# Newton steps and query rotation of the latent heads moved from VectorE to GpSimd, and half of a projection moved ahead of twelve transposes

## The chip, the cores and the metric

The kernel runs on one core of one Trainium2 chip. The metric is the device time of one execution in microseconds. Its engines have the profile's names: PE is TensorE, DVE is VectorE, ACT is ScalarE, POOL is GpSimd, SP issues the loads.

## What is computed

A trunk of two layers over 512 tokens of 1,024 features, all in float32. Layer 0 has two attentions side by side (differential attention, "A", with 4 heads, and latent attention, "B", with 8 heads), layer 1 has stick-breaking attention with 16 heads, and each layer ends with a SwiGLU network. The change lies in layer 0. Cut to that:

```python
a_q, a_k, a_v, b_ql, b_kvl, b_kr = split_cols(h @ w_in, AB_IN_SPLITS)
a_q = rope(rms_norm(a_q.reshape(B, S, 2 * A_HEADS, A_QK_DIM), a_q_norm), pos)
a_k = rope(rms_norm(a_k.reshape(B, S, 2 * A_HEADS, A_QK_DIM), a_k_norm), pos)
...
q_b = (rms_norm(b_ql, b_q_a_norm) @ b_w_q_b).reshape(B, S, B_HEADS, B_NOPE_DIM + B_ROPE_DIM)
kv_b = (rms_norm(b_kvl, b_kv_a_norm) @ b_w_kv_b).reshape(B, S, B_HEADS, B_NOPE_DIM + B_V_DIM)
q_nope, q_rope = q_b[..., :B_NOPE_DIM], q_b[..., B_NOPE_DIM:]
k_nope, b_v = kv_b[..., :B_NOPE_DIM], kv_b[..., B_NOPE_DIM:]
q_nope = rms_norm(q_nope, b_q_nope_norm)
k_nope = rms_norm(k_nope, b_k_nope_norm)
q_rope = rope(rms_norm(q_rope, b_q_rope_norm), pos)
out_b = latent_attention(q_nope, q_rope, k_nope, k_rope, b_v, (B_NOPE_DIM + B_ROPE_DIM) ** -0.5)
```

`rms_norm` divides by the root of a mean square, `rope` turns pairs of elements by an angle that depends on the token. B's q has 64 elements without rotation and 32 with it, per head.

## The kernel before

**Matmuls in three passes.** Every float32 operand is held as a rounded part (`_hi`) and a rest (`_lo`), and a product is hi*hi + hi*lo + lo*hi. The weights come in chunks g = 0, 1, 2, ...: SP loads a chunk into `wraw`, ACT writes `w_hi` (`hi_static`, line 318), POOL writes the rest `w_lo` (`lo(g)`, line 330), PE reads both. There are three slots, so ACT may split chunk g once PE is done with g-3 (a semaphore count), and SP may load chunk g once `w_lo` of g-3 is written. Chunks 4 and 5 are A's first q projection, 6 to 9 are B's two up-projections, 10 to 19 are A's other projections.

**Order.** The order of each engine is written out by hand, and engines meet by semaphores. An engine that waits holds back all that stands behind it. PE's order in layer 0 is: the latents (`lat_pe`), the first half of A's first projection (`pj_pe(pe, 0, 0, i)`, i counts four blocks of 128 tokens), twelve transposes of the normalised latents (`lat_trans_pe`, line 732, which wait for DVE's `latn`), the second half (`pj_pe(pe, 0, 1, i)`), then B's projections `bq_pe` and `bkv_pe` for heads 0 to 3 and again for heads 4 to 7, A's second projection `pj_pe(pe, 1, ...)` with the transposes of head 0's q and k between its halves (`b_qk_pe`, lines 1112 and 1119). Then comes a loop over the eight latent heads u: scores (`b_scores_pe`, line 1037), transposes of q and k of head u+1, three quarters of a half projection for A, transposes of the probabilities (line 1017), the last quarter, and values (line 1088). Then follow the four heads of A (scores at line 1167), the output projection, the network and layer 1.

**Beside it, in a head.** DVE takes the row maxima (`b_max_dve`, line 1050), ACT the exponentials (line 1054), DVE three reciprocals (`b_inv_dve`, line 1060), ACT scales the probabilities (line 1066) and splits q and k of the next head, DVE writes their rests (`b_qk_dve`) and those of the transposed probabilities (`b_pt_dve`, line 1080). `qk_dve` (lines 964 to 967) turns A's projections out of PSUM, t = 0 and t = 1 being the two banks; PE's next projection waits for its line 966 before it writes the same bank. `b_mean_dve` and `qk_mean_dve` (line 987) write mean squares.

**Norm factors.** 1/sqrt(m) is Ln and Exp on ACT (`rs_act`) and one Newton step on DVE, three small instructions (`rs_newton_dve`, lines 400, 402, 404). All norms share the scratch columns `T_M`, `T_Y` and `T_A` of `tiny`. The fourteen norms are numbered by `ROOT`, in order lat, b0, b1, q0, k0, k1, q1, o0, ...

**Pairs of latent heads.** B's q and k are scaled and q is turned for two heads at a time, before PE transposes them. `b_pair_dve` (lines 884 to 892) has five DVE instructions for the rotated 32 columns of q: two products with the sine table into `t2b`, one with the cosine table in place, a sum and the scale. `b_pair_pool` (line 905) has two POOL instructions for the 64 plain columns of q and of k. Pair 0 stands before the loop, pair n+1 at the end of DVE's work for head u = 2n, that is ahead of the maxima of head u+1:

```python
for c in range(3):
    b_pt_dve(dve, u, c)
...
if u % 2 == 0 and u < 6:
    b_pair_dve(dve, u // 2 + 1)
```

PE waits for both halves of a pair in `b_qk_pe`, right behind the scores of head 2n+1.

Of the kernel before, what the change touches and what calls it, by code (L numbers as in the profile page):

```python
# [140 lines left out]
def trunk(nc, xt, w_ab, w_in, w_down, mats, masks_a, masks_c, tabs, rows, vecs, out):  # L141
# [728 lines left out]
    def b_pair_dve(dve, pr):  # L870

        hf, h, z = pr // 2, 2 * pr, Z_B[pr // 2] + 8 * (pr % 2)
        dve.wait_ge(S("rs_root"), ROOT[f"b{hf}"] + 1)
# [15 lines left out]
        dve.wait_ge(S("b_rope"), 4 * pr + 3)
        nc.vector.tensor_tensor(q[:, :, :, c:B_QK], q[:, :, :, c:B_QK], t, ALU.add).then_inc(S("b_rope"), 1)  # L890
        dve.wait_ge(S("b_rope"), 4 * pr + 4)
        nc.vector.tensor_tensor(q[:, :, :, c:B_QK], q[:, :, :, c:B_QK], root(32, B_ROPE),
                                ALU.mult).then_inc(S("b_qk"), 1)

    def b_pair_pool(pool, pr):

# [1387 lines left out]
```

## Time and profile before

| what | value |
|---|---|
| median of three runs | 1336.61 us (1335.61 to 1336.84) |
| the profiled execution, its time | 1336.34 us |
| its span in the trace | 1334.5 us |
| PE busy | 1281.6 us (96%) |
| DVE, ACT, POOL busy | 598.0, 574.6, 514.0 us |
| mean granted clock of PE | 0.986 of full speed |

Times in the text are microseconds from the start of the span. A matmul's busy time overlaps its neighbour's, so PE's pace is read from the distance of two starts. The stretches are: latents and first projections to 75.9, the eight latent heads from there to 190.9, A's heads and the output projection to about 300, and the rest of the kernel, untouched by the change.

### The profile page before, as it was taken

What the parts mean: (1) busy time and instruction counts of PE and PEld (TensorE: products, weight loads), DVE (VectorE), ACT (ScalarE), POOL (GpSimd) and SP (SyncE); (2) the same over time, 40 slices, a digit from 0 to 9 for tenths busy, and PEclk for the clock granted to TensorE, in tenths of its full rate; (3) what the DMA queues carried; (4) which work ended last, traced back from release to release, by engine and by line L of the source; (5) the groups of instructions that cost most, each with busy time, mean ns of one, the idle gap of its engine ahead of it and who ended that gap; (6) DMA issues with size and microseconds to landing.
All of it is one profiled execution on the core that took longest, in us unless ns stands there. A gap on an engine that the chain in (4) does not pass through costs nothing.

```text
span 1334.5 us, 16920 instructions
## 1 busy us (share of the span) xinstructions
PE 1281.6 (96%) x6308; PEld 1076.2 (81%) x6308; DVE 598.0 (45%) x1033; ACT 574.6 (43%) x953; POOL 514.0 (39%) x223
## 2 busy tenths in 40 slices
PE   8888898999999999999989999998999999999999
PEld 8788887778888888888868888886888888888887
DVE  7877777753221112222168888887222220122210
ACT  5656665643332122233366777776333331222310
POOL 5432411164445434445522222221644453344441
PEclk9889998999999999999989999999999999999999
DMA  5220111022223222233111111110323332233331
GB/s 207 72 64 33 33 47 33 16 91 95 95 101 115 84 79 94 94 118 103 65 62 48 47 63 47 49 61 17 104 88 98 98 122 89 71 98 100 102 129 40
DMA packets 29143, 105.84 MB, mean 79 GB/s; under 512 B 3360, under 2 KB 3616, under 8 KB 29088
## 3 DMA queue, kind: packets, MB, share of 16 engines
q1 hardware_dynamic: 28944, 105.07, 23.9%
q8 instruction: 37, 0.61, 0.2%
q14 instruction: 18, 0.15, 0.0%
q10 hardware_dynamic: 144, 0.02, 0.0%
HBM read 102.98 MB, written 2.10 MB: 79 GB/s over the span
## 4 chain that ended last, share of the span: by engine, by line
PE 66%; DVE 17%; ACT 10%; issue 5%; POOL 1%; DMA 0%; ACTq 0%; DVEq 0%; SPq 0%; POOLq 0%
PE bank L342 19%; PE bank L343 19%; PE bank L346 19%; DVE cs_hi L1477 2%; DVE cs_lo L1479 2%; ACT ca L1435 1%; ACT ca L1433 1%; ACT w_hi L318 1%; ACT cq_hi L1516 1%; DVE pt_lo L1080 1%; POOL ssum L436 1%; ACT pn L1066 1%; ACT pn L1054 1%; DVE cs L1445 1%; DVE tiny L1185 1%
## 5 line engine op out<-in xcount | busy, mean ns | idle before, releaser
L330 POOL TENSOR_TENSOR w_lo<-wraw,w_hi 128x1024 fp32r<-128x1024 f32 (+4 forms) x180 | 458.6, 2549 | 751.8 <-ACT w_hi L318 751.8
L342 PE MATMUL bank<-h_hi,w_hi 128*128 128x512 f32 x896 | 353.8, 395 | 1.0 <-DVE h_lo L426 1.0
L343 PE MATMUL bank<-h_lo,w_hi 128*128 128x512 f32 x896 | 351.6, 392 | 0.0
L318 ACT ACTIVATE w_hi<-wraw 128x1024 fp32r<-128x1024 f32 (+4 forms) x180 | 197.3, 1096 | 158.2 <-DVE x L633 128.7
L346 PE MATMUL bank<-h_hi,w_lo 128*128 128x512 f32 x896 | 223.4, 391 | 0.0
L342 PEld LDWEIGHTS bank<-h_hi,w_hi 128*128 128x128 f32 x896 | 168.9, 188 | 38.6 <-DVE h_lo L426 1.6
L346 PEld LDWEIGHTS bank<-h_hi,w_lo 128*128 128x128 f32 x896 | 168.3, 188 | 37.0
L343 PEld LDWEIGHTS bank<-h_lo,w_hi 128*128 128x128 f32 x896 | 168.9, 189 | 36.0
L342 PE MATMUL bank<-f_hi,w_hi 128*128 128x512 f32 x352 | 138.3, 393 | 0.0
L343 PE MATMUL bank<-f_lo,w_hi 128*128 128x512 f32 x352 | 138.3, 393 | 0.0
L619 DVE TENSOR_TENSOR fu<-bank,rstd 128x512 f32<-128x512 f32 x44 | 30.4, 691 | 200.3 <-PE bank L346 200.3
L633 DVE TENSOR_TENSOR x<-bank,x 128x512 f32<-128x512 f32 x32 | 22.1, 692 | 202.2 <-PE bank L346 202.2
L596 ACT ACTIVATE f_hi<-fa 128x512 f32 (+1 forms) x44 | 27.8, 632 | 195.6 <-DVE fa L622 195.6
L592 ACT ACTIVATE fs<-fy 128x512 f32<-128x512 f32 x44 | 27.8, 632 | 138.3 <-DVE fy L617 138.3
L346 PE MATMUL bank<-f_hi,w_lo 128*128 128x512 f32 x352 | 86.4, 393 | 0.0
L343 PEld LDWEIGHTS bank<-f_lo,w_hi 128*128 128x128 f32 x352 | 66.2, 188 | 15.0
L346 PEld LDWEIGHTS bank<-f_hi,w_lo 128*128 128x128 f32 x352 | 66.2, 188 | 15.0
L342 PEld LDWEIGHTS bank<-f_hi,w_hi 128*128 128x128 f32 x352 | 66.2, 188 | 14.9
L617 DVE TENSOR_TENSOR fy<-bank,rstd 128x512 f32<-128x512 f32 x44 | 30.4, 691 | 104.6 <-PE bank L346 104.1
L930 PE MATMUL bank<-w_hi,h_hi 128*128 128x256 f32 x192 | 57.6, 300 | 5.2 <-DVE ka L966 4.8
L932 PE MATMUL bank<-w_hi,h_lo 128*128 128x256 f32 x192 | 55.5, 289 | 0.0
L934 PE MATMUL bank<-w_lo,h_hi 128*128 128x256 f32 x192 | 55.5, 289 | 0.0
(272 smaller groups left out, 2015.9 us busy)
## 6 DMA issues: line engine op xcount, KB each, us to landing
wraw<-in_w_in SPq DMA_DIRECT2D x120, 512.0 KB, 3.3
wraw<-in_w_down SPq DMA_DIRECT2D x32, 704.0 KB, 4.1
wraw<-in_w_ab SPq DMA_DIRECT2D x20, 512.0 KB, 3.3
x<-in_xt SPq DMA_DIRECT2D x8, 256.0 KB, 6.9
out<-x SPq DMA_DIRECT2D x8, 256.0 KB, 2.0
wraw<-in_w_ab SPq DMA_DIRECT2D x4, 416.0 KB, 6.8
wraw<-in_w_ab SPq DMA_DIRECT2D x2, 384.0 KB, 3.1
wraw<-in_w_ab SPq DMA_DIRECT2D x2, 256.0 KB, 2.9
```

The costliest lines, as they stand in the source:

```text
L318: nc.scalar.activation(whi[:, s, 0:width], wraw[:, s, 0:width], ACT.Copy).then_inc(S("w_hi"), 1)
L330: nc.gpsimd.tensor_tensor(wlo[:, s, 0:width], wraw[:, s, 0:width], whi[:, s, 0:width], ALU.subtract).then_inc(S("w_lo"), 1)
L342: nc.tensor.matmul(out_bank, w, src_hi[kt], start=(kt == 0), stop=False)
L343: nc.tensor.matmul(out_bank, w, src_lo[kt], start=False, stop=False)
L346: last = nc.tensor.matmul(out_bank, wlo[:, s, kt * P:(kt + 1) * P], src_hi[kt], start=False, stop=(kt == n - 1))
L592: nc.scalar.activation(fs[:], fy[:], ACT.Silu).then_inc(S("net_s"), 1)
L596: nc.scalar.activation(tile_at(f_of[L][0], f), as3(fa[:], f), ACT.Copy).then_inc(S("net_hi"), 1)
L617: nc.vector.tensor_tensor(fy[:], bank[2 * j][:], rstd[:], ALU.mult).then_inc(S("net_y"), 1)
L619: nc.vector.tensor_tensor(fu[:], bank[2 * j + 1][:], rstd[:], ALU.mult).then_inc(S("net_u"), 1)
L930: nc.tensor.matmul(o, tok(hhi, 4 * c + k, i), whi[:, slot(g), w], start=(c == 0 and k == 0 and i % 2 == 0), stop=False, skip_group_check=True)
L932: nc.tensor.matmul(o, tok(hlo, 4 * c + k, i), whi[:, slot(g), w], start=False, stop=False, skip_group_check=True)
L934: last = nc.tensor.matmul(o, tok(hhi, 4 * c + k, i), wlo[:, slot(g), w], start=False, stop=(c == 1 and k == 3), skip_group_check=True)
```

## The change

Three edits. GpSimd makes the Newton step of b0, b1, q0, k0, k1 and q1, in four instructions instead of three. GpSimd does the five instructions for q's rotation, in front of the two that it did already. PE runs the token blocks 0 and 1 of the second half of A's first projection ahead of the latents' transposes. With this, the steps get new places on POOL and DVE: on POOL, pair 0 comes before chunk 11's `w_lo` as it did, pairs 1 to 3 now come before chunk 14, 16 and 18 instead of behind them; on DVE, in heads 2 and 4 (and 6 for `va_dve`) the step for A's projection stands behind the first of the three reciprocals instead of behind the third. The writers of the means wait until the Newton step before theirs is done, since they share the scratch columns.

```diff
...
     def rs_newton_dve(dve, name, n, at):
         r = ROOT[name]
         m, y, a = (tiny[:, t:t + n] for t in (T_M, T_Y, T_A))
+        n_before = 2 * (r if r < ROOT["b0"] else r - len(POOL_ROOTS))
         dve.wait_ge(S("rs_exp"), r + 1)
+        wait(dve, "rs_root", r)
...
+    POOL_ROOTS = ("b0", "b1", "q0", "k0", "k1", "q1")
+
+    def rs_newton_pool(pool, name, n, at):
+        r, i = ROOT[name], 3 * POOL_ROOTS.index(name)
+        m, y, a = (tiny[:, t:t + n] for t in (T_M, T_Y, T_A))
+        pool.wait_ge(S("rs_exp"), r + 1)
+        pool.wait_ge(S("rs_root"), r)
+        nc.gpsimd.tensor_tensor(a, m, y, ALU.mult).then_inc(S("rs_pool"), 1)
+        pool.wait_ge(S("rs_pool"), i + 1)
+        nc.gpsimd.tensor_tensor(a, a, y, ALU.mult).then_inc(S("rs_pool"), 1)
+        pool.wait_ge(S("rs_pool"), i + 2)
+        nc.gpsimd.tensor_scalar(a, a, -0.5, 1.5, ALU.mult, ALU.add).then_inc(S("rs_pool"), 1)
+        pool.wait_ge(S("rs_pool"), i + 3)
+        nc.gpsimd.tensor_tensor(tiny[:, at:at + n], a, y, ALU.mult).then_inc(S("rs_root"), 1)
...
     def b_mean_dve(dve, hf):
         dve.wait_ge(S("bq_sum"), NB * hf + NB)
         dve.wait_ge(S("bk_sum"), NB * hf + NB)
+        dve.wait_ge(S("rs_root"), ROOT[f"b{hf}"])
...
     def b_pair_pool(pool, pr):
...
+        wait(pool, "b_rope", 4 * pr)
...
+        nc.gpsimd.tensor_tensor(t[:, :, :, 0:s], q[:, :, :, c + s:B_QK], tab(B_ROPE, s), ALU.mult).then_inc(S("b_rope"), 1)
+        nc.gpsimd.tensor_tensor(t[:, :, :, s:B_ROPE], q[:, :, :, c:c + s], tab(B_ROPE + s, s),
+                                ALU.mult).then_inc(S("b_rope"), 1)
+        pool.wait_ge(S("b_rope"), 4 * pr + 2)
+        nc.gpsimd.tensor_tensor(q[:, :, :, c:B_QK], q[:, :, :, c:B_QK], tab(0, B_ROPE), ALU.mult).then_inc(S("b_rope"), 1)
+        pool.wait_ge(S("b_rope"), 4 * pr + 3)
+        nc.gpsimd.tensor_tensor(q[:, :, :, c:B_QK], q[:, :, :, c:B_QK], t, ALU.add).then_inc(S("b_rope"), 1)
+        pool.wait_ge(S("b_rope"), 4 * pr + 4)
+        nc.gpsimd.tensor_tensor(flat(qb, c, B_QK), flat(qb, c, B_QK), root(32, B_ROPE), ALU.mult).then_inc(S("b_qk"), 1)
+        nc.gpsimd.tensor_tensor(flat(qb, 0, c), flat(qb, 0, c), root(0, c), ALU.mult).then_inc(S("b_nope"), 1)
+        nc.gpsimd.tensor_tensor(flat(kb, 0, c), flat(kb, 0, c), root(16, c), ALU.mult).then_inc(S("b_nope"), 1)
...
             lo(10)
+            rs_newton_pool(pool, "b0", 48, Z_B[0])
             b_pair_pool(pool, 0)
-            for g in range(11, 14):
-                lo(g)
+            lo(11)
+            rs_newton_pool(pool, "b1", 48, Z_B[1])
+            lo(12)
+            lo(13)
 
             for u in range(B_HEADS):
-                lo(14 + u)
                 if u % 2 == 0 and u < 6:
                     b_pair_pool(pool, u // 2 + 1)
+                lo(14 + u)
+                if u == 1:
+                    rs_newton_pool(pool, "q0", 16, Z_Q)
...
-                for c in range(3):
-                    b_inv_dve(dve, u, c)
+                b_inv_dve(dve, u, 0)
                 if u in (2, 4):
                     qk_dve(dve, 1 + u // 2, 1)
                 if u == 6:
                     va_dve(dve, 4, 1)
+                for c in range(1, 3):
+                    b_inv_dve(dve, u, c)
...
-                if u % 2 == 0 and u < 6:
-                    b_pair_dve(dve, u // 2 + 1)
...
+            for i in range(2):
+                pj_pe(pe, 0, 1, i)
             pe.wait_ge(S("lam_exp"), 1)
             lat_trans_pe(pe)
-            for i in range(NB):
+            for i in range(2, NB):
                 pj_pe(pe, 0, 1, i)
```

What this makes of the order on POOL, from chunk 10's `w_lo` to chunk 13's, before (line 905 is the pair's two scales):

```order
L330 TENSOR_TENSOR w_lo<-wraw,w_hi 128x1024
L905 TENSOR_TENSOR qb<-qb,tiny 128x8x64
L905 TENSOR_TENSOR kb<-kb,tiny 128x512
L330 TENSOR_TENSOR w_lo<-wraw,w_hi 128x1024 x4
L905 TENSOR_TENSOR qb<-qb,tiny 128x8x64
```

and now (lines 415 to 421 are a Newton step, 907 to 917 a pair):

```order
L330 TENSOR_TENSOR w_lo<-wraw,w_hi 128x1024
L415 TENSOR_TENSOR tiny<-tiny 128x48
L417 TENSOR_TENSOR tiny<-tiny 128x48
L419 TENSOR_SCALAR tiny<-tiny 128x48
L421 TENSOR_TENSOR tiny<-tiny 128x48
L907 TENSOR_TENSOR t2b<-qb,tbq 128x8x16
L908 TENSOR_TENSOR t2b<-qb,tbq 128x8x16
L911 TENSOR_TENSOR qb<-qb,tbq 128x8x32
L913 TENSOR_TENSOR qb<-qb,t2b 128x8x32
L915 TENSOR_TENSOR qb<-qb,tiny 128x8x32
L916 TENSOR_TENSOR qb<-qb,tiny 128x8x64
L917 TENSOR_TENSOR kb<-kb,tiny 128x512
```

Nine more instructions stand between chunk 10's `w_lo` and chunk 11's, which PE needs for the half projection behind head 0's transposes.

On DVE, between the last rest of head 0's probabilities (`b_pt_dve`) and the maxima of head 1, before:

```order
L1080 TENSOR_TENSOR pt_lo<-bank,pt_hi 128x384 [waits h_phi] x2
L884 TENSOR_TENSOR t2b<-qb,tbq 128x8x16 [waits bq_ev,rs_root]
L885 TENSOR_TENSOR t2b<-qb,tbq 128x8x16
L888 TENSOR_TENSOR qb<-qb,tbq 128x8x32 [waits b_rope]
L890 TENSOR_TENSOR qb<-qb,t2b 128x8x32 [waits b_rope]
L892 TENSOR_TENSOR qb<-qb,tiny 128x8x32 [waits b_rope]
L1050 TENSOR_REDUCE tiny<-bank 128x2 [waits h_s]
```

and now:

```order
L1092 TENSOR_TENSOR pt_lo<-bank,pt_hi 128x512 [waits h_phi]
L1092 TENSOR_TENSOR pt_lo<-bank,pt_hi 128x384 [waits h_phi] x2
L1062 TENSOR_REDUCE tiny<-bank 128x2 [waits h_s]
L1113 TENSOR_TENSOR mixed_lo<-bank,mixed_hi 64x512 [waits h_mhi]
L1062 TENSOR_REDUCE tiny<-bank 128x1 [waits h_s] x2
```

The maxima of head 1 have nothing of the pair ahead of them any more.

## Rows read from the trace of the kernel before

**Rows 1.** The page, part 1: busy time, share of the span, instructions.
```profile
PE 1281.6 (96%) x6308; PEld 1076.2 (81%) x6308; DVE 598.0 (45%) x1033; ACT 574.6 (43%) x953; POOL 514.0 (39%) x223
```

**Rows 2.** Waits of PE, 60 to 191: total us, times, longest us.
```profile
PE bank L1112 <- DVE qb L892: 5.9, 3, 3.8
PE bank L930 <- DVE ka L966: 4.8, 2, 2.6
PE bank L818 <- DVE vb_lo L858: 2.4, 1, 2.4
```

**Rows 3.** Timeline of PE: start, us, instruction, idle before and its releaser.
```profile
35.98 2.79 PE L732 MATMUL bank<-mat,latn 128*128 128x128 f32 x12 [3.18 <-DVE latn L712]
94.54 1.09 PE L1112 MATMUL bank<-mat,qb 128*96 128x128 f32 x4 [3.76 <-DVE qb L892]
```

**Rows 4.** Busy time by stretch; behind POOL's: granted PE clock, DMA share, GB/s.
```profile
36.00:41.80 5.80, 5.80 (x28) 5.80 (x29) 4.47 (x11) 3.66 (x6) 3.09 (x2) 0.50 0.15 47
60.90:63.30 2.40, 0.04 (x2) 0.00 (x1) 2.33 (x9) 1.50 (x6) 2.01 (x3) 1.00 0.49 140
94.50:99.70 5.20, 5.16 (x25) 4.99 (x26) 2.71 (x8) 4.51 (x14) 0.00 (x0) 0.50 0.00 0
145.80:147.90 2.10, 2.10 (x13) 2.10 (x13) 0.54 (x2) 0.87 (x2) 0.00 (x0) 0.56 0.00 0
```

**Rows 5.** Timeline of PE: chunk 11's start; first scores of heads 0, 1, 7, A.
```profile
70.34 0.37 PE L930 MATMUL bank<-w_hi,h_hi 128*128 128x256 f32 x1
...
75.88 0.28 PE L1037 MATMUL bank<-bk_hi,bq_hi 96*128 96x256 f32 x1
...
88.19 0.28 PE L1037 MATMUL bank<-bk_hi,bq_hi 96*128 96x256 f32 x1
...
177.25 0.28 PE L1037 MATMUL bank<-bk_hi,bq_hi 96*128 96x256 f32 x1
...
190.91 0.28 PE L1167 MATMUL bank<-ak_hi,aq_hi 128*128 128x256 f32 x1
```

**Rows 6.** Timeline of DVE: a step of b0's Newton, a sum, pair 1.
```profile
58.87 2.30 DVE L402 TENSOR_TENSOR tiny<-tiny 128x48 f32<-128x48 f32 x1
...
78.03 0.68 DVE L967 TENSOR_REDUCE tiny<-pj_sq 128x8 f32<-128x512 f32 x1
...
87.16 2.48 DVE L885 TENSOR_TENSOR t2b<-qb,tbq 128x128 f32<-128x128 f32 x1
89.67 1.15 DVE L888 TENSOR_TENSOR qb<-qb,tbq 128x256 f32<-128x256 f32 x1
...
92.04 2.45 DVE L892 TENSOR_TENSOR qb<-qb,tiny 128x256 f32<-128x256 f32 x1
```

**Rows 7.** Timeline of POOL.
```profile
58.64 2.46 POOL L330 TENSOR_TENSOR w_lo<-wraw,w_hi 128x1024 fp32r<-128x1024 f32 x1 [3.11 <-ACT w_hi L318]
61.49 1.04 POOL L905 TENSOR_TENSOR qb<-qb,tiny 128x512 f32<-128x512 f32 x1 [0.39 <-DVE tiny L404]
...
77.75 2.38 POOL L330 TENSOR_TENSOR w_lo<-wraw,w_hi 128x1024 fp32r<-128x1024 f32 x1 [6.82 <-ACT w_hi L318]
86.90 2.59 POOL L330 TENSOR_TENSOR w_lo<-wraw,w_hi 128x1024 fp32r<-128x1024 f32 x1 [6.77 <-ACT w_hi L318]
...
90.50 1.22 POOL L905 TENSOR_TENSOR kb<-kb,tiny 128x512 f32<-128x512 f32 x1
```

**Rows 8.** POOL's groups by shape, 0 to 300: busy us, mean ns, idle before.
```profile
L1628 POOL TENSOR_TENSOR tq<-rawt,rawg 128x512 f32<-128x512 f32 x1 | 1.3, 1295 | 0.0
...
L1628 POOL TENSOR_TENSOR tbq<-rawt,rawg 128x256 f32<-128x256 f32 x1 | 0.7, 717 | 0.0
```

**Rows 9.** Timeline of DVE and ACT where A's first projection is turned.
```profile
43.77 0.42 DVE L964 TENSOR_TENSOR t<-bank,tq 128x256 f32<-128x256 f32 x1 [1.59 <-ACT pj_sq L945]
...
45.04 0.68 DVE L967 TENSOR_REDUCE tiny<-pj_sq 128x8 f32<-128x512 f32 x1
...
47.50 0.49 ACT L833 ACTIVATE bq_sq<-bank 128x384 f32<-128x384 f32 x1
```

More of the change, by code:

```diff
@@ L868, in b_mean_dve, with b_pair_pool @@
                                        spread(col(T_EPS), [P, 16]), ALU.mult, ALU.add).then_inc(S("rs_mean"), 1)
-    def b_pair_dve(dve, pr):
+    def b_pair_pool(pool, pr):
         hf, h, z = pr // 2, 2 * pr, Z_B[pr // 2] + 8 * (pr % 2)
-        dve.wait_ge(S("rs_root"), ROOT[f"b{hf}"] + 1)
-        dve.wait_ge(S("bq_ev"), NB * hf + NB)
+        pool.wait_ge(S("rs_root"), ROOT[f"b{hf}"] + 1)
+        pool.wait_ge(S("bq_ev"), NB * hf + NB)
+        pool.wait_ge(S("bk_ev"), NB * hf + NB)
+        wait(pool, "b_rope", 4 * pr)
         q = qb[:, h:h + 2, :, :]
@@ L889, in b_pair_dve @@
[L889 to L897, printed above, removed]
-        hf, h, z = pr // 2, 2 * pr, Z_B[pr // 2] + 8 * (pr % 2)
-        pool.wait_ge(S("rs_root"), ROOT[f"b{hf}"] + 1)
-        pool.wait_ge(S("bq_ev"), NB * hf + NB)
-        pool.wait_ge(S("bk_ev"), NB * hf + NB)
-        for t, at in ((qb, 0), (kb, 16)):
-            o = t[:, h:h + 2, :, 0:B_NOPE].rearrange("p h i n -> p (h i) n")
-            nc.gpsimd.tensor_tensor(o, o, spread(col(z + at, 8).rearrange("p (j o) -> p j o", o=1), [P, 8, B_NOPE]),
-                                    ALU.mult).then_inc(S("b_nope"), 1)
+            return spread(col(z + at, 8).rearrange("p (j o) -> p j o", o=1), [P, 8, n])
@@ new lines, in flat @@
+        def flat(t, a, b):
+            return t[:, h:h + 2, :, a:b].rearrange("p h i n -> p (h i) n")
+        nc.gpsimd.tensor_tensor(t[:, :, :, 0:s], q[:, :, :, c + s:B_QK], tab(B_ROPE, s), ALU.mult).then_inc(S("b_rope"), 1)
+        nc.gpsimd.tensor_tensor(t[:, :, :, s:B_ROPE], q[:, :, :, c:c + s], tab(B_ROPE + s, s),
+                                ALU.mult).then_inc(S("b_rope"), 1)
+        pool.wait_ge(S("b_rope"), 4 * pr + 2)
+        nc.gpsimd.tensor_tensor(q[:, :, :, c:B_QK], q[:, :, :, c:B_QK], tab(0, B_ROPE), ALU.mult).then_inc(S("b_rope"), 1)
@@ L984, in qk_mean_dve @@
         dve.wait_ge(S("pj_sum"), 2 * p + 2)
+        dve.wait_ge(S("rs_root"), ROOT[GROUPS[p]])
         e, n = ((T_EQ, A_DIM * A_SCALE ** 2), (T_E, A_DIM))[p // 2]
@@ L1300, in a_omean_dve @@
         dve.wait_ge(S("a_l0"), u + 1)
+        dve.wait_ge(S("rs_root"), ROOT[f"o{u}"])
         nc.vector.scalar_tensor_tensor(col(T_M, NB), bank[TRK][:, 0:NB], 1.0 / (2 * A_DIM), col(T_L0, NB), ALU.mult,
@@ L1643, in _ @@
             lo(10)
+            rs_newton_pool(pool, "b0", 48, Z_B[0])
             b_pair_pool(pool, 0)
-            for g in range(11, 14):
-                lo(g)
+            lo(11)
+            rs_newton_pool(pool, "b1", 48, Z_B[1])
+            lo(12)
+            lo(13)
             for u in range(B_HEADS):
-                lo(14 + u)
                 if u % 2 == 0 and u < 6:
                     b_pair_pool(pool, u // 2 + 1)
+                lo(14 + u)
+                if u == 1:
+                    rs_newton_pool(pool, "q0", 16, Z_Q)
+                elif u in (3, 5):
+                    rs_newton_pool(pool, ("k0", "k1")[u // 4], 16, Z_K + 16 * (u // 4))
+                elif u == 7:
+                    rs_newton_pool(pool, "q1", 16, Z_Q + 16)
                 if u == 0:
@@ L1933, in _ @@
                     b_pt_dve(dve, u, c)
[L1934 to L1938 removed]
+                if u == 6:
                     qk_mean_dve(dve, 1)
[L1940 to L1942 removed]
                 if u in (1, 3):
```

18 lines of the change are left out of this document (2 added, 16 removed).

## The prediction

> **What bounds the kernel now.** I read the page's first part, then PE's waits by stretch, then the timelines of the engines around each wait. PE is busy 96% of the span [rows 1], so a gain can only come from its idle time, and from stretches in which its clock is at half. The reader is to see in [rows 2] that PE lost 13.1 us in the stretch of the latent heads and just before it to three causes, all on DVE: q's rotation 5.9 (line 892), the bank of A's projection 4.8 (line 966), and B's values 2.4 (line 858). Another 3.18 went at 32.8, where the transposes wait for the normalised latents [rows 3]. A long wait costs more than itself: after those of 3.18 and 3.76 [rows 3] PE ran for 5.8 and 5.2 us at a granted clock of 0.50, its lower level of 1.2 GHz, and did half the work it could have: 2.9 and 2.6 us lost. After the wait of 2.4 the clock had stayed at 1.00; a stretch at 0.56 near 146 cost some 0.9 [rows 4].
>
> Why DVE is late is in [rows 6, 7]. Pair 1's step at line 885 took 2.48 us and ended at 89.64, when POOL's `w_lo` (86.90 + 2.59 = 89.49) was done. Line 888 took 1.15 beside POOL's scale, line 892 took 2.45. A step of b0's Newton took 2.30 and ended at 61.17, POOL's instruction at 61.10. So a DVE instruction with both inputs in SBUF is held until the running POOL instruction ends. The maxima of head 1 wait behind all that.
>
> **Edit 1: Newton and rotation leave DVE.** DVE loses four pairs (pair 1 took from 87.16 or sooner to 92.04 + 2.45 = 94.49, 7.3 us) and six Newton steps, of which one instruction alone took 2.30 [rows 6]. What comes instead on POOL: the tables give 1.295 us for 512 columns and 0.717 for 256 [rows 8], so 2.26 ns a column and 0.14 fixed. The rotation is 2 x 0.43 (128 columns) and 3 x 0.72 (256), 3.0, and with three waits on itself (estimate 0.13 each) 3.4. The two scales were there (1.04 each, [rows 7]), so a pair takes 5.5. A Newton step of 48 columns is 4 x 0.25 plus waits, 1.5.
>
> Where it lies on the path, place by place.
>
> *Before head 0.* Chunk 10's `w_lo` ends at 61.10 [rows 7]. Then come Newton 1.5 (62.6), pair 0 5.5 (68.1) and chunk 11's `w_lo` 2.4: PE may start chunk 11 at 70.5. It started it at 70.34 [rows 5]. So what PE wins of the 2.4 us at 60.9, since DVE has b0's step no more, it waits for on POOL: **+0.2**. This term hangs on POOL alone, and the rotation is in it in full. Bounds: -0.5, if the patterns of 16 columns run at the rate of the scales, and +3, if they are twice as dear as the tables.
>
> *Pair 1.* It starts after chunk 13's `w_lo` (77.75 + 2.38 = 80.1, [rows 7]) and ends at 85.6. PE asks for it at 94.54 - 3.76 = 90.8 [rows 3]: 5.2 us to spare. Pairs 2 and 3 start behind the Newton step of an odd head, and are asked for behind the scores of the next odd one, with more to spare. So no wait on the rotation is left, and the chunks of `w_lo` behind the pairs are used a head later.
>
> *The heads.* From head 0 to A's first scores it took 190.91 - 75.88 = 115.0 us [rows 5]. Head 0, with no real wait, took 88.19 - 75.88 = 12.3, the last 13.7. With seven heads at 12.3 and the last at 13.7, less 0.5 for DVE's late start into it (POOL held q1's Newton too), it is 86.1 + 13.2 = 99.3: 15.7 us less. The waits and the half clock, added up another way, give 5.9 + 4.8 + 2.6 + 0.9 = 14.2, and restarts and maxima that came late make the rest. What is late next: in heads 2 and 4 A's turning (lines 964 to 967, 45.72 - 43.77 = 1.95 us, [rows 9]) now stands ahead of two reciprocals, and ACT's scaling waits for them, just before PE wants the probabilities. I put 0.3 a head and keep 0.9 for three heads (bounds 0 and 4). The term is **-14.8**, bounds -15.7 and -10.
>
> The added waits of DVE for a Newton step on POOL (`b_mean_dve`, `qk_mean_dve`, `a_omean_dve`) come at least a head after that step; b1's mean waits for b0's step, done by 62.6, some 3 us before its sums are. I cost them at nothing. If POOL's step is late there, ACT, which waits for the mean, is held with all that stands behind it.
>
> **Edit 2: two token blocks ahead of the transposes.** A half projection took 75.88 - 70.34 = 5.5 us [rows 5], so half of one is 2.8, and fills the wait of 3.18 [rows 3] but for 0.4. The clock should stay up, the transposes take half of their 2.79, and PE is done with the projection at 36.0 + 1.4 + 2.8 = 40.2, some 5 us sooner, and with the first two blocks of `bq_pe` (12 matmuls of 384 columns, 0.17 each) at 42.3. The third waits for ACT's square (line 833, 47.50 + 0.49, [rows 9]). ACT gets there behind the second square of A's projection, which shares a buffer with the first and so waits for DVE's line 967 (45.72). DVE can do its four steps 1.59 sooner [rows 9], perhaps 2, so ACT's square ends near 46.2 instead of 47.99. PE then has waited 3.9 us, as long as the waits after which its clock fell. At half clock the next 5 us of matmuls cost 2.6, which eats the 1.8 and more, of which ACT's queue hides some. The term is **+0.4**, bounds -2.3 (clock stays up) and +1. The wait is moved, not removed.
>
> Loads: DMA and SP are off the path, chunk 14 is loaded after chunk 11's `w_lo` at 70.5 and its own `w_lo` starts at 86.90 [rows 7], so nothing hangs on SP's queue. Past 191 nothing changes but the start.
>
> **Sum.** +0.2 - 14.8 + 0.4 = -14.2 on the profiled execution's own 1336.34. The median of the runs is 1336.61, 0.27 higher; the same change on it gives **1322.4**.
>
> **Where a rule speaks against it.** The rows have DVE and POOL exclude each other: POOL's own scale went from 1.04 alone to 1.22 beside DVE's rotation [rows 7]. The Trainium skill (Perfetto Trace Analysis, Optimizing Scalar/DVE Operations) says that moving operations between these two might not help, because they share an SBUF read port. It would have the term of the heads mostly gone. Its page on SBUF (SBUF — State Buffer, Who interferes with whom) says that only DVE instructions with two SBUF inputs or in a two-port mode collide. By that, little is left on DVE to collide with, and the trace agrees: line 967, one SBUF input, took 0.68 beside POOL's `w_lo` at 77.75 and 0.68 without POOL at 45.04 [rows 6, 7, 9].
>
> **The rivals.**
> - *The wait moves with the work.* POOL, held by what DVE still does in SBUF and twice as slow a column, has pairs 1 to 3 ready no sooner than DVE had. Then the 5.9 us on line 892 and the 2.6 of half clock stay: -14.2 + 8.5 = -5.7, 1330.9. For it: POOL is the slower engine. Against it: 5.2 us to spare at pair 1. The skill's first rule above would end here.
> - *The clock stays up* in the wait at 42.2, or the wait is shorter than I work out: up to 2.7 more (from +0.4 to -2.3), 1319.7. For it: 2.4 us did not lower it. Against it: after 3.18 and 3.76 it was down.
> - *GpSimd becomes the bound (slower).* No row shows POOL on patterns of two heads by four tokens by 16 columns. If each such instruction costs e/5 more than I put, pair 0 passes all of e on to chunk 11, pair 1 what exceeds 5.2, pairs 2 and 3 what exceeds about 7, and waits as long as those in [rows 3] bring the half clock, 2.6 each. At e = 7.5 (a rotation instruction of 2.1 us instead of 0.6) the gain is used up. At e = 9 it is 9 + 3.8 + 4 + 5.2 = 22 against 14.2: 1344. Against it: the scales, in 8 rows of 64, are faster than the tables.
> - *Nothing changes*, because another engine takes the place of each wait: 1336.6. ACT and DVE are busy 43% and 45% of the span [rows 1], so it would have to come from the order, not from load.
>
> **Numbers.** Forecast 0.72, clock up 0.14, wait moves 0.08, GpSimd bound 0.04, nothing 0.02. The likeliest gives 1322.4. The range takes in the bounds of the forecast's terms to both sides without adding all of them up: low 1317.5 (clock up, no new wait in the heads, 0.5 at chunk 11), high 1328.5 (+3 at chunk 11 and 3 to 4 in the heads). A measurement of this kernel can tell about 0.2%, 2.7 us, from no change. Faster 0.94, same 0.02, slower 0.04.
>
> **What would show it.** In the changed profile: no wait of PE at the transposes of q (line 1112's successor) and at most traces of one on A's bank; heads 12.3 us apart, A's first scores near 177; a new wait of some 3.8 us in `bq_pe` near 42 with a clock of 0.50 behind it; chunk 11 started by PE near 70.5 right after POOL's `w_lo`; POOL's rotation instructions at 0.43 and 0.72. The prediction is wrong if a rotation instruction takes over 1.5 us, if the reciprocals behind A's turning hold the probabilities by more than 1 us a head, or if maxima are late for another reason.

## The result, and the profile after

The changed kernel took 1316.83 us (median of four runs, 1315.25 to 1319.36), the kernel before 1336.11 beside it: a ratio of 0.986 (95% interval 0.984 to 0.988), so faster by about 19 us. Two later series of the same kernel gave medians of 1319.3 and 1318.44, and the median of all twelve of its runs is 1318.44, so the first four lay low. The forecast was 1322.4, its range began at 1317.5.

The page, part 1, beside [rows 1]:

```profile
PE 1277.3 (97%) x6308; PEld 1073.8 (81%) x6308; DVE 567.6 (43%) x995; ACT 574.5 (44%) x953; POOL 529.4 (40%) x267
```

DVE lost 30.4 us of busy time, POOL gained 15.4. Twice as much came off one engine as went onto the other, and a good part of it was no work: the profile counts an instruction that is held as busy (2.48 us for one in [rows 6] whose like takes 0.28). The 13.1 us of waits of [rows 2] come down to two rows, by the timeline of PE (start, us, instruction, idle before and its releaser). All its rows with an idle time over 0.2 us from 30 to 165 are these:

```profile
35.54 1.50 PE L749 MATMUL bank<-mat,latn 128*128 128x128 f32 x12 [0.36 <-DVE latn L729]
45.57 0.69 PE L822 MATMUL bank<-w_hi,ql_hi 128*128 128x384 f32 x1 [3.71 <-ACT bq_sq L850]
...
62.32 0.50 PE L835 MATMUL bank<-w_hi,kvl_hi 128*128 128x512 f32 x1 [1.50 <-DVE vb_lo L875]
69.92 0.38 PE L941 MATMUL bank<-w_hi,h_hi 128*128 128x256 f32 x1 [0.32 <-POOL w_lo L330]
```

The wait at the transposes went from 3.18 [rows 3] to 0.36 and came back as 3.71 ahead of `bq_pe`'s third block. The one on B's values went from 2.4 to 1.50. Nothing is left on q's rotation, nor on A's bank. Clock and load by stretch (behind POOL's: granted clock, DMA share, GB/s), as in [rows 4]:

```profile
36.00:42.00 6.00, 5.86 (x46) 5.54 (x44) 5.09 (x11) 3.43 (x6) 3.18 (x2) 1.00 0.25 64
46.00:50.00 4.00, 4.00 (x15) 3.86 (x15) 1.66 (x7) 1.34 (x4) 0.65 (x1) 0.50 0.38 131
```

The stretch at the lower level (1.2 GHz) moved from behind the first wait to behind the second. POOL, from chunk 10's `w_lo` to chunk 11's, answers to [rows 7]:

```profile
58.54 2.40 POOL L330 TENSOR_TENSOR w_lo<-wraw,w_hi 128x1024 fp32r<-128x1024 f32 x1 [3.62 <-ACT w_hi L318]
60.90 0.28 POOL L415 TENSOR_TENSOR tiny<-tiny 128x48 f32<-128x48 f32 x1
...
61.95 0.28 POOL L421 TENSOR_TENSOR tiny<-tiny 128x48 f32<-128x48 f32 x1
62.31 0.46 POOL L907 TENSOR_TENSOR t2b<-qb,tbq 128x128 f32<-128x128 f32 x1
...
64.08 0.74 POOL L913 TENSOR_TENSOR qb<-qb,t2b 128x256 f32<-128x256 f32 x1
64.90 0.62 POOL L915 TENSOR_TENSOR qb<-qb,tiny 128x256 f32<-128x256 f32 x1
...
67.48 2.39 POOL L330 TENSOR_TENSOR w_lo<-wraw,w_hi 128x1024 fp32r<-128x1024 f32 x1
```

The Newton step took 1.41 us from start to start, the pair 5.17 (62.31 to 67.48). PE starts chunk 11 at 69.92, when POOL is done (69.87), so this place does hang on POOL. From chunk 10's `w_lo` to chunk 11's start it is 11.38 us, against 11.70 before. A's first scores:

```profile
173.92 0.28 PE L1179 MATMUL bank<-ak_hi,aq_hi 128*128 128x256 f32 x1
```

They started at 190.91 [rows 5], 16.99 later. From here to the end it is 1143.58 us, before it was 1143.59. Head 0's first scores are at 75.49 (75.88 in [rows 5]). Those 0.4 us are not the change's. A's first projection, which starts ahead of everything that was changed, already starts 0.45 sooner in this trace (timeline of PE, the kernel before, then the changed one):

```profile
26.90 0.36 PE L930 MATMUL bank<-w_hi,h_hi 128*128 128x256 f32 x1
26.45 0.36 PE L941 MATMUL bank<-w_hi,h_hi 128*128 128x256 f32 x1
```

That start lies between 26.3 and 27.5 in the sixteen traces, with the change and without it. From it to head 0's first scores it is 48.98 us before and 49.04 now, so nothing was won there. The heads gave 16.6: 98.43 instead of 115.03. In the seven other traces with all three edits (e1, e8, e10, e11, e12, e13, e14), but for e10, they take 98.35 to 98.45.

### The profile page after: what moved, and what is told of

Read it like the earlier page. It is cut to its first block, busy times and chain, and to the rows that moved or that the text cites. A ratio compares the mean times of both kernels' runs of the same rounds, so it can differ in the third digit from the quotient of the medians.

```text
span 1317.5 us, 16942 instructions
## 1 busy us (share of the span) xinstructions
PE 1277.3 (97%) x6308; PEld 1073.8 (81%) x6308; DVE 567.6 (43%) x995; ACT 574.5 (44%) x953; POOL 529.4 (40%) x267
## 4 chain that ended last, share of the span: by engine, by line
PE 72%; DVE 12%; ACT 9%; issue 5%; POOL 1%; DMA 0%; ACTq 0%; DVEq 0%; POOLq 0%
PE bank L342 20%; PE bank L343 20%; PE bank L346 20%; DVE cs_hi L1490 2%; DVE cs_lo L1492 1%; ACT w_hi L318 1%; ACT ca L1448 1%; ACT ca L1446 1%; PE bank L1100 1%; PE bank L941 1%; PE bank L945 1%; PE bank L943 1%; PE bank L1049 1%; ACT cq_hi L1529 1%; PE bank L1029 1%
## 5 line engine op out<-in xcount | busy, mean ns | idle before, releaser
L636 DVE TENSOR_TENSOR fu<-bank,rstd 128x512 f32<-128x512 f32 x44 | 30.4, 691 | 200.3 <-PE bank L346 200.3
L634 DVE TENSOR_TENSOR fy<-bank,rstd 128x512 f32<-128x512 f32 x44 | 30.4, 691 | 104.6 <-PE bank L346 104.2
L435 ACT ACTIVATE h_hi<-x,vec 128x512 fp32r<-128x512 f32 x32 | 23.0, 717 | 71.0 <-DVE x L650 40.8
```

The costliest lines, as they stand in the source:

```text
L634: nc.vector.tensor_tensor(fy[:], bank[2 * j][:], rstd[:], ALU.mult).then_inc(S("net_y"), 1)
L636: nc.vector.tensor_tensor(fu[:], bank[2 * j + 1][:], rstd[:], ALU.mult).then_inc(S("net_u"), 1)
```

## The experiments

The theory: DVE's two-input SBUF instructions and POOL's long ones shut each other out, and what was won is DVE's time beside POOL's, in the order in which the two engines were set. Rivals: it is load (DVE has less to do); or it is edit 2 and the clock; or the reordering of reciprocals and chunks did it. The kernels compute what the reference computes. Only the two with a delay have products added, into scratch that is overwritten.

**e1_again: the changed kernel once more.** No edit.

> The changed kernel once more, with a second profile. Its four times lie 4.1 us apart (1315.25 to 1319.36), before's 2.5 apart. Theory A (the clock decides): the wait of 3.7 us in the second up-projection near 45.6 lowers the clock in some executions only, so a profile with a time near 1316 shows a granted clock near 1.00 from 46 to 50 and one near 1319 shows 0.50 there. Theory B (the spread has nothing to do with that wait): the clock there is 0.50 again whatever the time, and the difference lies in other stretches, first of all behind 300.

Measured: 1319.3 (1317.4 to 1319.76), ratio 0.988 [0.986, 0.989]. The trace gives 0.50 at 46 to 50 and 0.59 at 50 to 52 (0.73 in the first). So the time behind one and the same wait differs between executions.

**e2_no_early: edit 2 undone.**

```diff
-            for i in range(2):
-                pj_pe(pe, 0, 1, i)
             pe.wait_ge(S("lam_exp"), 1)
             lat_trans_pe(pe)
-            for i in range(2, NB):
+            for i in range(NB):
```

> The changed kernel with edit 2 undone: all four token blocks of the second half projection behind the transposes. Theory A (my term of +0.4 was right, and the surprise is all in the heads): within 1 us of the changed kernel, wait of 3.2 back at 35.9, no wait at 45.6, head 0 within 0.5 of 75.5. Theory B (the blocks ahead of the transposes won what I did not count): 2 to 3 us slower than the changed kernel.

**e3_only_early: the kernel before with edit 2 alone** (the same lines, put into it).

> The kernel before with edit 2 alone. Theory A: within 1 us of before (0.9993 to 1.0007), the 3.2 us wait at 36 replaced by one of 3.7 at 46 with the clock at 0.50 behind it. Theory B: 2 to 3 us faster than before.

Measured: without edit 2 1318.27 (1317.72 to 1319.02), 0.988 [0.986, 0.989]; edit 2 alone 1337.56 (11 runs), 1.0013 [1.0004, 1.0023]. So edit 2 wins nothing in one setting and costs 1.8 us in the other. The traces say that it costs: from the start of A's first projection to head 0's first scores it is 47.35 us without it (e2_no_early), and 48.05 to 49.20 in the changed kernel and its like (the trace above, e1, e4, e10, e14). Part of the 1.8 us is the clock, which in e3_only_early's trace fell behind the wait of 2.52 at 62.5 (0.62 from 62 to 66), and in the kernel before stayed at 1.00 behind its 2.35. PE's timeline of edit 2 alone shows the wait moved as in the changed kernel, with the others in their places:

```profile
35.55 1.50 PE L732 MATMUL bank<-mat,latn 128*128 128x128 f32 x12 [0.36 <-DVE latn L712]
45.58 0.45 PE L805 MATMUL bank<-w_hi,ql_hi 128*128 128x384 f32 x1 [3.70 <-ACT bq_sq L833]
...
62.53 0.50 PE L818 MATMUL bank<-w_hi,kvl_hi 128*128 128x512 f32 x1 [2.52 <-DVE vb_lo L858]
```

**e4_recips_first: the three reciprocals together again, ahead of A's turning.**

```diff
-                b_inv_dve(dve, u, 0)
+                for c in range(3):
+                    b_inv_dve(dve, u, c)
                 if u in (2, 4):
                     qk_dve(dve, 1 + u // 2, 1)
...
-                for c in range(1, 3):
-                    b_inv_dve(dve, u, c)
```

> The changed kernel with the three reciprocals together again, A's turning behind them in heads 2, 4 and 6. Theory A (the new place costs nothing and wins nothing, since PE has other work until the probabilities are there): within 0.5 us of the changed kernel. Theory B (the new place is part of the gain: PE's bank for A's third block comes free in time only with it): 0.3 us a head of wait on A's bank come back in heads 2 and 4, 0.6 to 1 us slower. Theory C (my forecast's 0.9 us loss was real and hidden in the sum): 0.9 faster.

Measured: 1318.38, 0.987 [0.986, 0.989], the same as the changed kernel. The two waits on A's bank come back with 0.7 us in sum (waits of PE, 60 to 180: total us, times, longest):

```profile
PE bank L941 <- DVE ka L977: 0.7, 2, 0.3
```

By the traces the eight heads take 98.87 us with the reciprocals first and 98.43 in the changed kernel, so the reordering is good for 0.4 us, too little for the medians to tell. The rest of the 4.8 us on that bank [rows 2] is not the reordering's: 2.7 of it come back with the Newton steps on DVE (e6 below), none with the rotation there (e5).

**e5_newton_only and e6_rotation_only: one part of edit 1 alone**, edit 2 kept in both. In the first the rotation is back on DVE, in the second the Newton steps.

```diff
...
             b_mean_dve(dve, 1)
+            b_pair_dve(dve, 0)
...
+                if u % 2 == 0 and u < 6:
+                    b_pair_dve(dve, u // 2 + 1)
...
-            rs_newton_pool(pool, "b0", 48, Z_B[0])
...
+            rs_newton_dve(dve, "b0", 48, Z_B[0])
...
```

(The first two places are e5_newton_only: `b_pair_dve` has the five instructions again, `b_pair_pool` keeps the two scales, at the changed kernel's places. The last two are e6_rotation_only, and likewise for the other five norms.)

> The changed kernel with the rotation back on DVE, at its old places; the Newton steps stay on GpSimd. Theory A (what costs is DVE standing ahead of the maxima while a GpSimd instruction holds it): the waits on the rotation come back, 5.9 us on PE with a half clock behind pair 1, and A's bank too in the odd heads stays won, since the Newton steps of DVE were what made it late in heads 2 and 4. About 9 to 10 us slower than the changed kernel, 1327. Theory B (Newton steps alone carry the gain): within 2 us of the changed kernel. Theory C (rotation alone carries it): close to before, 1334 or more.

> The changed kernel with all Newton steps back on DVE at their old places; the rotation stays on GpSimd. Theory A: the waits on A's bank (4.8 us in heads 2 and 4) come back in part, since b_max starts late behind a Newton step held by chunk 15's, 17's `w_lo`; the wait of 2.4 at 61 is back and the wait on chunk 11 gone. 4 to 6 us slower than the changed kernel, 1323. Theory B of e5: close to before. Theory C of e5: within 2 us of the changed kernel.

Measured: Newton alone 1328.88, 0.995 [0.994, 0.997]; rotation alone 1324.63, 0.992 [0.990, 0.994]. As shares of the time before that is 0.5% and 0.8%, together 1.3%, and both at once gave 1.2%: within the intervals the two parts add up, neither makes up for the other. With the rotation on DVE (e5), PE waits for it as before (waits of PE, 60 to 191):

```profile
PE bank L1131 <- DVE qb L910: 7.0, 3, 2.3
```

and DVE's timeline shows why:

```profile
86.54 0.27 DVE L902 TENSOR_TENSOR t2b<-qb,tbq 128x128 f32<-128x128 f32 x1
86.73 2.47 DVE L903 TENSOR_TENSOR t2b<-qb,tbq 128x128 f32<-128x128 f32 x1
89.24 2.47 DVE L906 TENSOR_TENSOR qb<-qb,tbq 128x256 f32<-128x256 f32 x1
91.75 0.42 DVE L908 TENSOR_TENSOR qb<-qb,t2b 128x256 f32<-128x256 f32 x1
```

Two of the instructions take 2.47, their like without POOL 0.27 and 0.42. With the Newton steps on DVE (e6), it is a step of b0's:

```profile
58.50 2.44 DVE L400 SCALAR_TENSOR_TENSOR tiny<-tiny 128x48 f32<-128x48 f32 x1
60.97 0.21 DVE L402 TENSOR_TENSOR tiny<-tiny 128x48 f32<-128x48 f32 x1
```

and the wait on B's values is back at 2.5, that on A's bank at 2.7.

**e7_pool_waits and e9_scales_first: the kernel before, with only POOL's order changed.** Nothing leaves DVE. In both, POOL waits until DVE's rotation is done before it starts the next `w_lo`; in e9_scales_first it also makes its own two scales first.

```diff
             for u in range(B_HEADS):
-                lo(14 + u)
                 if u % 2 == 0 and u < 6:
                     b_pair_pool(pool, u // 2 + 1)
+                    pool.wait_ge(S("b_qk"), u // 2 + 2)
+                lo(14 + u)
...
```

(That is e9_scales_first; e7_pool_waits has the wait alone ahead of `lo(14 + u)`, and the scales behind it as they were.)

> The kernel before, with one line more: in heads 0, 2 and 4 GpSimd waits for DVE's rotation of the next pair before it starts the chunk's `w_lo`. Nothing is moved between engines. Theory A (the lock of the two engines is the cost, not the 2 us of work on DVE): DVE's five instructions take 2.1 us instead of 6.3 to 7.5, PE's 5.9 us on line 892 shrink to under 1.5, and the kernel is 6 to 9 us faster than before, 1328. Theory B (it is the amount of work on DVE that makes it late): under 2 us faster than before.

> The kernel before with GpSimd's order changed alone: in heads 0, 2 and 4 the next pair's two scales come first, then it waits for DVE's rotation, then the chunk's `w_lo`. e7 had the scales behind `w_lo`, so PE waited for them instead. Theory A (the lock is the cost): rotation on DVE under 2.2 us, PE's wait on the pairs under 1 us in all, no half clock behind pair 1, kernel 8 to 10 us faster than before, 1327, though no work has changed engines. Theory B (DVE's load is the cost): 2 us faster, as e7.

Measured: e7_pool_waits 1333.42 (10 runs), 0.9985 [0.9975, 0.9994]; e9_scales_first 1328.52, 0.995 [0.993, 0.996]. DVE's timeline of e9_scales_first, pair 1:

```profile
87.09 0.27 DVE L884 TENSOR_TENSOR t2b<-qb,tbq 128x128 f32<-128x128 f32 x1
87.29 0.28 DVE L885 TENSOR_TENSOR t2b<-qb,tbq 128x128 f32<-128x128 f32 x1
87.60 0.42 DVE L888 TENSOR_TENSOR qb<-qb,tbq 128x256 f32<-128x256 f32 x1
...
88.52 0.42 DVE L892 TENSOR_TENSOR qb<-qb,tiny 128x256 f32<-128x256 f32 x1
```

The five instructions take 1.85 us (87.09 to 88.94), against 7.3 and more in [rows 6]. So the rotation was never 7 us of work. It was less than 2 us of work and over 5 of being shut out. e7_pool_waits had the same 1.85, and yet won only 0.15%: now POOL's own scales stood behind `w_lo`, and PE waited for those (6.5 us in three waits on line 1112, for which the profile names no releaser; for pair 1 POOL's second scale ends at 94.16 and PE starts at 94.26). And in e9_scales_first `w_lo`, held back to 89.03, pushes the instruction behind it, POOL's sum for `qa` (line 974), onto the next victim, a mean of 16 columns. POOL, then DVE:

```profile
91.37 2.39 POOL L974 TENSOR_TENSOR qa<-qa,t 128x1024 f32<-128x1024 f32 x1
91.75 2.04 DVE L987 SCALAR_TENSOR_TENSOR tiny<-tiny 128x16 f32<-128x16 f32 x1
```

with PE's waits on A's bank up from 4.8 to 6.1. Order alone gives about 7 of the 17 us, less than the 8 to 10 expected. For these 7 load is not the cause, since DVE does in e9_scales_first all that it did before. For the other 10 it is argued and not shown: no run took all of the holding away and left the work on DVE.

**e10_delay_late and e11_delay_first: the changed kernel with POOL held up**, by six products into the scratch `t2b`, once ahead of each of pairs 1 to 3, once ahead of pair 0.

```diff
                 if u % 2 == 0 and u < 6:
...
+                    for k in range(6):
+                        nc.gpsimd.tensor_tensor(t2b[:], ..., ALU.mult)...
...
                     b_pair_pool(pool, u // 2 + 1)
```

> The changed kernel with six more GpSimd instructions of 0.74 us (products of the sine table, 4.9 us with their waits) ahead of pairs 1, 2 and 3. Theory A (these pairs have over 5 us to spare, as forecast): within 1 us of the changed kernel. Theory B (GpSimd is near its limit in the heads, and its queue would soon be the bound): 3 us or more slower.

> The changed kernel with the same 4.9 us ahead of pair 0 alone. Theory A (pair 0 and chunk 11's `w_lo` are on the path with nothing to spare): PE waits 3 to 5 us at head 0's transposes and at chunk 11, 4.6 to 5 us slower, and up to 2.6 more if the clock falls, so 1323 to 1326. Theory B (spare here as in the heads): within 1 us.

Measured: e10_delay_late 1317.97 (1316.9 to 1319.29), in its times no different from the changed kernel; e11_delay_first 1324.62, 0.991 [0.990, 0.993], some 6 us slower than it. The six products took 4.1 us each time. PE's timeline of e11_delay_first (its first wait is for pair 0, whose last instruction ends at 71.45 on POOL; the profile names no releaser):

```profile
71.56 1.06 PE L1124 MATMUL bank<-mat,qb 128*96 128x128 f32 x4 [2.96 <-issue]
73.82 0.58 PE L941 MATMUL bank<-w_hi,h_hi 128*128 128x256 f32 x1 [0.35 <-POOL w_lo L330]
```

and the stretch behind the wait:

```profile
71.50:76.00 4.50, 4.10 (x18) 3.54 (x19) 1.49 (x2) 1.36 (x2) 4.25 (x6) 0.50 0.27 78
```

Chunk 11 starts 3.9 us later (73.82 against 69.92), and the half clock behind the wait makes the loss larger than the delay (first scores at 81.39 against 75.49). Pair 0 is on the path in full, pairs 1 to 3 have over 4 us to spare: PE never waits for them in e10_delay_late. Yet the delay was not free in its trace. The heads took 99.43 us and not 98.4, all of it in head 5 (12.99 against 11.95). There POOL's sum for `ka` (line 985), pushed back by the delay, runs beside DVE's mean, which takes 0.16 in the changed kernel:

```profile
138.87 2.39 POOL L985 TENSOR_TENSOR ka<-ka,t 128x1024 f32<-128x1024 f32 x1
138.91 2.38 DVE L999 SCALAR_TENSOR_TENSOR tiny<-tiny 128x16 f32<-128x16 f32 x1
```

So to move POOL's work in time, even where PE has room for it, can set it beside another two-input instruction of DVE.

**e8_act_early: to remove the wait that edit 2 left.** ACT, which held PE at 45.57, makes the first two squares of `bq` between those of A's projection.

```diff
-            for t in range(2):
-                qk_act(act, 0, t)
+            qk_act(act, 0, 0)
+            for i in range(2):
+                bq_act(act, 0, i)
+            qk_act(act, 0, 1)
             hi_static(act, 8)
-            for i in range(NB):
+            for i in range(2, NB):
```

> The changed kernel, and ACT takes the first two blocks of B's up-projection between the two squares of A's first projection instead of behind them. Theory A (the wait of 3.7 us that edit 2 moved to the up-projection is ACT's order, and hangs on nothing else): the wait is gone, the clock stays at 1.00 from 42 to 55, the next wait is 2 to 3 us near 47 on B's values, and the kernel is 2.5 to 3.5 us faster than the changed kernel. Theory B (DVE's order is the limit there): under 1 us.

Measured: 1317.77 (1317.1 to 1318.3), 0.987 [0.985, 0.988]. The wait went from ACT to DVE and stands 5 us further on (timeline of PE):

```profile
50.70 0.80 PE L835 MATMUL bank<-w_hi,kvl_hi 128*128 128x512 f32 x1 [3.02 <-DVE vb_lo L875]
```

DVE has one instruction behind the other from 45.0 to 50.8, apart from 0.6 us: the stretch is bound by it, and reordering ACT moves the wait only. From the start of A's first projection head 0's first scores come after 46.91 us, 1.1 to 2.3 sooner than with the changed kernel's order (48.05 to 49.20), but this trace also started 1.0 later than the first one, and the medians do not tell the two kernels apart.

**e12_act_l0: e8_act_early, and a tiny product out of the lock's way.** The kernel before and the changed one share a collision that the change did not touch, in A's head 0. In the changed kernel's trace DVE had

```profile
185.60 0.75 DVE L1222 SCALAR_TENSOR_TENSOR pn<-e,tiny,pn 128x512 f32<-128x512 f32 x1
186.27 2.31 DVE L1226 SCALAR_TENSOR_TENSOR tiny<-tiny 128x4 f32<-128x4 f32 x1
188.50 0.68 DVE L1361 TENSOR_TENSOR x<-bank,x 128x512 f32<-128x512 f32 x1
```

and POOL

```profile
185.69 2.87 POOL L330 TENSOR_TENSOR w_lo<-wraw,w_hi 128x1024 fp32r<-128x1024 f32 x1 [9.64 <-ACT w_hi L318]
```

Four columns take 2.31 us. PE waits 1.6 us for `x` (line 1361) behind it. Here the product is moved ahead of the last combination (line 1222):

```diff
+        if c == 2:
+            l0 = tiny[:, T_L:T_L + 8:2]
+            nc.vector.scalar_tensor_tensor(col(T_L0, NB), l0, EPS, l0, ALU.mult, ALU.mult).then_inc(S("a_l0"), 1)
         for k in range(b, b + n):
...
-        if c == 2:
...
```

> e8 and one thing more: in A's heads DVE writes the small product of the sums (`T_L0`) ahead of the last combination of probabilities instead of behind it. In the changed kernel it took 2.3 us there beside chunk 22's `w_lo`, and the output projection's bank waited 1.6 us for DVE. Theory A (same lock, same cure): the wait of 1.6 at 189 is gone, the kernel 1.5 us faster than e8, and up to 2 more if the clock then stays up from 189 to 197. Theory B (another DVE step is held instead): as e8.

Measured: 1315.54 (1314.6 to 1318.52), 0.986 [0.984, 0.987]. The lock took the instruction that now stood there, the combination itself, which PE waits for directly (4.1 instead of 1.9 us):

```profile
183.81 2.90 DVE L1225 SCALAR_TENSOR_TENSOR pn<-e,tiny,pn 128x512 f32<-128x512 f32 x1
```

From A's first scores to line 428 it is 28.34 us, and 28.82 in e8_act_early, so the move itself gave 0.5 us. Of the 3.5 us between the two spans 2.3 lie behind 280, where the edit moves nothing: there the clock stayed up in this trace (below).

**e13_lo_after_l0: e8_act_early, and POOL waits instead.** Its chunk in A's head u starts when DVE's product is done. PE needs the chunk much later.

```diff
             for u in range(A_HEADS):
+                pool.wait_ge(S("a_l0"), u + 1)
                 lo(22 + u)
```

> e8, and in A's heads GpSimd waits for DVE's small product of the sums (line 1226) before it writes chunk 22's to 25's `w_lo`, which PE needs two heads later. e12 moved that product, and the lock caught the large combination behind it (2.90 us). Theory A (the lock is the cost in A's head 0 too): DVE's product and combination take 0.17 and 0.75, PE's waits there are 1.9 and under 0.3 instead of 1.9 and 1.6, the clock stays at 1.00 from 186 to 196, and the kernel is 3 to 4 us faster than e8, 1314. Theory B (PE waits there for something else as well): within 1 us of e8.

Measured: 1309.46 (five runs, 1309.05 to 1310.22), ratio 0.981 [0.979, 0.982]: 8.3 us less than e8_act_early, over twice what was expected, and the fastest of all. DVE's timeline:

```profile
183.06 0.75 DVE L1222 SCALAR_TENSOR_TENSOR pn<-e,tiny,pn 128x512 f32<-128x512 f32 x1
183.73 0.15 DVE L1226 SCALAR_TENSOR_TENSOR tiny<-tiny 128x4 f32<-128x4 f32 x1
183.80 0.68 DVE L1361 TENSOR_TENSOR x<-bank,x 128x512 f32<-128x512 f32 x1
```

and POOL's, held for a moment and done long before it is needed:

```profile
183.97 2.39 POOL L330 TENSOR_TENSOR w_lo<-wraw,w_hi 128x1024 fp32r<-128x1024 f32 x1 [10.44 <-DVE tiny L1226]
```

The clock behind it, in the changed kernel

```profile
188.00:192.00 4.00, 2.67 (x6) 2.17 (x7) 3.94 (x7) 0.59 (x2) 0.56 (x1) 0.50 0.38 135
192.00:196.00 4.00, 4.00 (x16) 3.36 (x15) 1.44 (x3) 0.00 (x0) 0.00 (x0) 0.69 0.00 0
```

and in e13_lo_after_l0

```profile
184.00:188.00 4.00, 4.00 (x23) 3.47 (x24) 3.94 (x8) 2.03 (x5) 2.36 (x1) 1.00 0.17 46
188.00:192.00 4.00, 4.00 (x33) 3.92 (x31) 1.72 (x5) 1.40 (x3) 0.00 (x0) 1.00 0.22 89
```

Against e8_act_early the spans differ by 8.1 us (1316.5 and 1308.4): 1.4 ahead of the latent heads (first scores at 74.37 and 72.99), 4.3 in A's head 0 (from line 1222's last row to the next head's first, 18.77 and 14.42), and 2.4 behind 240. Only the 4.3 lie where the edit acts: 1.6 is the wait for `x`, the rest goes with the half clock that followed it. From the transposes of the probabilities to line 428 PE takes 12.0 us here, and 15.4 to 16.7 in the fourteen traces that have the collision. The other two are places where the clock fell in one trace and not in the other, behind waits of equal length (below). Yet all five runs lie 6.9 us or more below all four of e8_act_early, so this is no chance of one trace; whether the edit has a part in it was not tried, and the cause of these 3.8 us stays open. One instruction of four columns, held for 2.2 us, was worth a quarter of the 17 us that the whole change gained.

**e14_again: the changed kernel in the same series as e13_lo_after_l0.**

> The changed kernel a third time. Theory A (its usual time is near 1318, and the first four runs, median 1316.83, lay low by chance; two of my missing 5.6 us are that): median 1317.5 to 1319. Theory B (the first median is its usual time): under 1317.

Measured: 1318.44 (1317.06 to 1319.93), 0.988 [0.986, 0.989]. So e13_lo_after_l0 beats it by 9.0 us on the same chip, and the intervals are far apart. Its clock was down behind the wait near 280 as in the first trace of the changed kernel (0.64 at 282 to 286), so it isn't the chip that keeps it up in e13_lo_after_l0. In e12_act_l0, on another chip, it was 1.00 there too.

## Where the prediction held, and the step that failed

**Direction and mechanism: right.** The waits on line 892 and on A's bank are gone, chunk 11 hangs on POOL alone, pairs 1 to 3 have room, and A's part to the end took the same time. That DVE and POOL shut each other out was read from [rows 6, 7], and e5, e6, e7, e9 and e13 show it.

**The size: 5.6 us short on the medians, and 0.67 below the range.** The step that failed is the term of the heads, -14.8: it measured -16.6, outside its own bounds. On the profiled executions the forecast was 1336.34 - 14.2 = 1322.1 and the time 1319.36, so 2.8 us are missing. They are, from the traces:
- *The heads, 1.8.* "Seven heads at 12.3" were 12.33, 11.97, 12.38, 11.96, 12.39, 11.95 and 11.97, 84.95 us in sum and not 86.1: I took head 0, the one head seen without a wait, for all, and it is one of the long kind. The last was 13.48, not 13.2. The 0.9 us kept for A's turning ahead of the reciprocals did not occur: with the old order (e4) heads 2 and 4 are 0.2 us longer, not shorter. In sum -1.15 + 0.28 - 0.9 = -1.8. Every head runs the same number of matmuls and transposes, 94. The long kind loses 0.2 us at the transposes of the probabilities and 0.2 at the values; why was not tried.
- *Chunk 11, 0.5.* Forecast +0.2, measured -0.3 (11.38 us instead of 11.70 from chunk 10's `w_lo`). The Newton step took 1.41 instead of 1.5 and the pair 5.17 instead of 5.5, and the bound in which 16 columns at a time cost twice as much did not come.
- *Edit 2, nothing.* Forecast +0.4, and in this trace chunk 10's `w_lo` starts 0.35 later behind the start of A's first projection than before (32.09 and 31.74). The wait of 3.9 worked out for it was 3.71, its clock 0.50. It does reach chunk 11: with edit 2 chunk 10's `w_lo` starts 31.1 to 32.3 us behind that start (e1, e4, e10, e11, e14 and this trace), without it 30.4 (e2), and chunk 11 follows 11.4 behind it each time, but where e11 delays it.
- *The start, 0.45*, which is not the change's. The other 2.8 of the 5.6 lie between the profiled executions and the medians, and the median of these four runs lay low: by all twelve runs the miss is 4.0.
- *The range.* It followed the terms of one execution, and had nothing for the spread of the time itself. Its low end is close to the sum of all favourable bounds (-0.5 - 15.7 - 2.3 = -18.5, so 1318.1). The same kernel gave medians of 1316.83, 1319.3 and 1318.44. By the later two the range would have held, though its largest term lay outside its own bounds in all three traces of this kernel (98.43, 98.43 and 98.35 us for the heads).
- *A reading.* "After the wait of 2.4 the clock had stayed at 1.00" rests on a row that covers the wait itself. It was so behind the wait too (1.00 from 62 to 66), but only in that execution: behind one of 2.52 at the same place it fell in e3, e7 and e9 (0.62, 0.66 and 0.59 from 62 to 66).

**The rivals.** *The wait moves with the work*: no. e10 gives pairs 1 to 3 4.1 us more, and PE does not wait for them. *The clock stays up*: no, 0.50 at 46 to 50; but what it pays is less than I had it, for in e8 and e13 the next wait (3.02) came anyway. *GpSimd becomes the bound*: at pair 0 it is the bound, with nothing to spare: e11 shows that each microsecond there costs one and a half. Its price of 0.6 an instruction was right (0.46 to 0.74), so nothing of this rival's extra cost came. *The rule that moving work between the two might not help* (the Trainium skill, Perfetto Trace Analysis, Optimizing Scalar/DVE Operations) did not hold here: 30.4 us less on DVE for 15.4 more on POOL, and 17 less in all. The condition on its SBUF page (the Trainium skill, SBUF — State Buffer, Who interferes with whom), that only DVE instructions with two SBUF inputs or in a two-port mode collide, agrees with what the runs show for two inputs: the rotation takes 1.85 us beside an idle POOL and over 7 beside `w_lo` and what follows it on POOL. No run here shows a two-port mode.

## What to carry to other kernels

When small instructions of DVE take over 2 us in a timeline and end together with one of POOL's, ask first which of the two has time to wait. One semaphore that lets POOL start behind them gave 4.3 us here by the traces, where moving the DVE instruction gave 0.5, because the next two-input instruction was caught instead. Look through what stands behind the held-back POOL instruction as well: it moves too, and in e9 and e10 it caught another of DVE's. Moving such work onto POOL pays where POOL has room and the chunk behind it is not yet asked for; put a price on the one place where it has none. And take the spread of the profiled execution into the range, and all iterations that the trace shows rather than the one without a wait.
